# Hybrid decoder layer on one core: how the low pieces of the attention weights are divided between VectorE and GpSimd

## The chip, the cores and the metric

The kernel runs on one core of a Trainium2 chip. The metric is the device time of one execution in microseconds (us), the median of several runs. Engines are TensorE (PE in the profile; PEld are its weight loads), VectorE (DVE), ScalarE (ACT), GpSimd (POOL) and SyncE (SP, which issues most DMAs).

## What is computed

One layer of a decoder over 4096 tokens of width 1024: a normed and modulated input is projected, its columns feed three mixers (forgetting attention with 8 heads of 64, an RWKV-7 recurrence, a pooling), and their gated outputs are projected back. The change lies in the attention alone, whose reference is:

```python
log_f = jax.nn.log_sigmoid((f_logit + f_bias).astype(jnp.float32))
cum = jnp.cumsum(log_f, axis=1).transpose(0, 2, 1)
for i in range(S // Q_BLOCK):                     # 32 blocks of 128 queries
    s = jnp.einsum('bhqd,bhkd->bhqk', qh[:, :, q0:L], kh[:, :, :L])
    s = s + cum[:, :, q0:L, None] - cum[:, :, None, :L]
    p = jax.nn.softmax(jnp.where(causal, s, -jnp.inf), axis=-1)
    outs.append(jnp.einsum('bhqk,bhkd->bhqd', p, vh[:, :, :L]))
```

## The kernel before

The program has five stages, one behind the other: `prepare`, `project`, `recur`, `attend` and `output`. `recur` also does the attention's first row maxima; `attend` lasts from about 1980 to 3147 us of the profiled span.

`attend` is a loop of four turns, each over two heads. A turn has 16 steps, (head u, block b of 512 queries), and step b has 4(b+1) units, one for each block x of 128 keys: 288 units in a turn. In a unit, `p32` holds exp of the scores, 128 keys x `width[k]` queries. The width is 512 but for the last three units of a step, which lie on the diagonal: 384, 256 and 128. Since every step starts at a multiple of four units, unit number modulo 4 says which diagonal width a unit can have: 1 is 384, 2 is 256, 3 is 128.

For precision the weights are multiplied in two pieces. The high piece is the upper half of each float32 of `p32`, read as bfloat16 in place; the low piece `plo` (float16) is `p32` minus the high piece. It is this subtraction that the change divides anew. In the kernel before, unit k's subtraction is done whole by GpSimd (L2711) unless k % 4 is 2, and then whole by VectorE (L2864, in `lower`).

The order of the work is written out by hand, by engine, with semaphores between them:

- TensorE, for unit k: (a mask on the diagonal, L2789), two products into the scores' bank `psc[k % 2]` (L2791, L2793), which wait for exp of unit k - 2; one product for the row maxima of queries 49 units ahead (L1396, four banks `pm`); sometimes a turned row of bounds (L2748); and then `output(k - 5)` (PV_LAG is 5): for each 128 queries one product with the high piece (L2772) and one with the low piece (L2774). `output` waits for the low piece. Right behind a step's start one `output` is skipped and two are done in the next unit.
- ScalarE: exp of each unit (L2732), and at a step's end two evacuations of the sums (L2724). `p32` and `plo` have eight buffers.
- VectorE, for unit k: perhaps the copy of a turned row (L2842), the maximum over the product for row maxima (L2834), `lower(k - 1)`, perhaps the largest of a row (L2847), and five and six units behind a step's start the result (L2870, L2872) and its scaling (L2877). Once a head, `head_vectors` (L1429 to L1433).
- GpSimd, for unit k: perhaps the sums of a row (L1403, which waits for VectorE's maxima of unit k - 1), perhaps a row's seven small pieces (L1412 to L1423, which wait for L2847), and then the low piece.

Of the kernel before, what the change touches and what calls it, by code (L numbers as in the profile page):

```python
# [23 lines left out]
ALU = mybir.AluOpType  # L24
# [4 lines left out]
P = 128  # L29
# [2538 lines left out]
def attend(nc, a, m):  # L2568
# [5 lines left out]
    with ExitStack() as ctx:  # L2574
# [10 lines left out]
        NP, NM = 8, 4  # L2585
        p32 = sb("p32", [P, NP, BT])
        plo = sb("plo", [P, NP, BT], F16)
# [10 lines left out]
        use, row_use, row_there, NPM, pre, EARLY, PV_LAG, ROW_LAG, COPY_LAG = (  # L2598
            p.use, p.row_use, p.row_there, p.NPM, p.pre, p.EARLY, p.PV_LAG, p.ROW_LAG, p.COPY_LAG)

        def by_pool(n):

            return n % 4 != 2

        pool_units = [k for k in range(NQK) if by_pool(k)]
        dve_units = [k for k in range(NQK) if not by_pool(k)]

        k_in = [sem(f"k_in{j}") for j in range(2)]
        q_in = [sem(f"q_in{j}") for j in range(2)]
# [16 lines left out]
        with nc.Block() as block:  # L2626
# [52 lines left out]
            @block.gpsimd  # L2679
            def _(pool):  # L2680
                pool.sem_inc(m_add.sem, EARLY)
                pool.sem_inc(piece.sem, 6 * EARLY)
                pool.sem_inc(row_d.sem, EARLY)
                with pool.Fori(0, TURNS) as i:
                    def sums(kc):

                        pool.wait_ge(pm_d.sem, pm_d.past(i, pre + use[kc] + len(ahead(kc))))
                        row_sum(nc, m, completes(kc)).then_inc(m_add.sem, 1)

                    def pieces(kc):  # L2690

                        nth = rows_before(kc + 1)
                        side, done = (nth - 1) % 2, nth - 1 - EARLY
                        pool.wait_ge(m_max.sem, m_max.past(i, done + 1))
                        for j in range(6):
                            row_piece(nc, m, j, side).then_inc(piece.sem, 1)
                            pool.wait_ge(piece.sem, piece.past(i, done * 6 + j + 1))
                        row_piece(nc, m, 6, side).then_inc(row_d.sem, 1)

                    for k in range(NQK):  # L2700
                        if complete_at(k - 1):
                            sums(k - 1)
                        if complete_at(k - 3):
                            pieces(k - 3)
                        if not by_pool(k):
                            continue
                        pool.wait_ge(exp_d.sem, exp_d.past(i, k + 1))
                        pool.wait_ge(pv_mm.sem, pv_mm.past(i, k + 1 - NP))
                        hi = p32[:, k % NP, :].bitcast(BF16).rearrange("p (t two) -> p t two", two=2)[:, :, 1]
                        w = width[k]  # L2710
                        nc.gpsimd.tensor_tensor(plo[:, k % NP, 0:w], p32[:, k % NP, 0:w], hi[:, 0:w], ALU.subtract)\  # L2711
                            .then_inc(lo_p.sem, 1)

# [24 lines left out]
            @block.tensor  # L2738
            def _(pe):
                pe.sem_inc(pv_mm.sem, pv_mm.credit)  # L2740
                pe.sem_inc(pm_mm.sem, pre)

                def turn_row(g, nth, side):

                    pe.wait_ge(row_d.sem, nth)
                    turned = pm[g][:, 0, :].bitcast(F16)
                    for t in range(CB):
                        ins = nc.tensor.transpose(turned[:, t * P:(t + 1) * P], mw[:, side, t, :], id16[:])  # L2748
                    ins.then_inc(pm_mm.sem, 1)


                with pe.Fori(0, TURNS) as i:
                    def output(k):

                        s, x = units[k]
                        u, b = STEPS[s]
                        if x == 0:
                            pe.wait_ge(o_ev.sem, o_ev.past(i, s))
                            if b == 0:
                                pe.wait_ge(v_in[u], (i + 1) * 16)  # L2760
                        if by_pool(k):
                            pe.wait_ge(lo_p.sem, lo_p.past(i, pool_units.index(k) + 1))
                        else:
                            pe.wait_ge(lo_v.sem, lo_v.past(i, dve_units.index(k) + 1))
                        d = max(0, x - 4 * b)
                        hi = p32[:, k % NP, :].bitcast(BF16).rearrange("p (t two) -> p t two", two=2)[:, :, 1]
                        for t in range(d, CB):
                            c0 = (t - d) * P
                            o = po[t // 2]
                            oc = (t % 2) * VW  # L2770

                            nc.tensor.matmul(o[:, oc:oc + VW], hi[:, c0:c0 + P], v[u][:, x, 0:VW],  # L2772
                                             start=(x == 0 and t % 2 == 0), stop=False, skip_group_check=True)
                            g = nc.tensor.matmul(o[:, oc:oc + 1 + HD], plo[:, k % NP, c0:c0 + P], v[u][:, x, 0:1 + HD],  # L2774
                                                 start=False, stop=(x == 4 * b + t), skip_group_check=True)
                        g.then_inc(pv_mm.sem, 1)

                    for k, (s, x) in enumerate(units):
                        u, b = STEPS[s]
                        if x == 0:  # L2780
                            pe.wait_ge(pm_d.sem, pm_d.past(i, pre + row_there(s) + 1))
                        d = max(0, x - 4 * b)
                        w = width[k]
                        t0 = b * BT + d * P
                        pe.wait_ge(exp_d.sem, exp_d.past(i, k + 1 - 2))
                        ks = slice(x * P, (x + 1) * P)
                        diag = x >= 4 * b
                        if diag:
                            nc.tensor.matmul(psc[k % 2][:, 0:P], idb[:], mk[:], start=True, stop=False,  # L2789
                                             skip_group_check=True)  # L2790
                        nc.tensor.matmul(psc[k % 2][:, 0:w], ka[u][:, ks], qa[u][:, t0:t0 + w], start=not diag,  # L2791
                                         stop=False, skip_group_check=diag)
                        nc.tensor.matmul(psc[k % 2][:, 0:w], kb[u][:, ks], qb[u][:, t0:t0 + w], start=False,  # L2793
                                         stop=True, skip_group_check=diag).then_inc(qk_mm.sem, 1)
                        for j, item in enumerate(ahead(k)):
                            ua, ba = STEPS[item[0]]
                            if ba == 0 and item[1] == 0:

                                nth = i + 1 if ua == 1 else i + 2
                                pe.wait_ge(q_in[ua], nth * 80)  # L2800
                                pe.wait_ge(k_in[ua], nth * 96)
                                pe.wait_ge(fac_in, 32)
                            n = pre + use[k] + j
                            pe.wait_ge(pm_d.sem, pm_d.past(i, n + 1 - NM))
                            query_maximum(nc, m, pm[n % NM][:, 0, :], qa[ua], ka[ua], item).then_inc(pm_mm.sem, 1)
                        if complete_at(k - ROW_LAG):
                            nth = rows_before(k - ROW_LAG + 1)
                            n = pre + use[k] + len(ahead(k))
                            pe.wait_ge(pm_d.sem, pm_d.past(i, n + 1 - NM))
                            turn_row(n % NM, i * NS + nth, (nth - 1) % 2)  # L2810
                        if k - PV_LAG in start[1:NS]:
                            continue
                        if k - (PV_LAG + 1) in start[1:NS]:
                            output(k - (PV_LAG + 1))
                        if k >= PV_LAG:
                            output(k - PV_LAG)
                    for k in range(NQK - PV_LAG, NQK):
                        output(k)

            @block.vector  # L2820
            def _(dve):
# [27 lines left out]
                with dve.Fori(0, TURNS) as i:  # L2849
# [6 lines left out]

                    def lower(k):

                        if not by_pool(k):
                            w = width[k]  # L2860
                            dve.wait_ge(exp_d.sem, exp_d.past(i, k + 1))
                            dve.wait_ge(pv_mm.sem, pv_mm.past(i, k + 1 - NP))
                            hi = p32[:, k % NP, :].bitcast(BF16).rearrange("p (t two) -> p t two", two=2)[:, :, 1]
                            tt(plo[:, k % NP, 0:w], p32[:, k % NP, 0:w], hi[:, 0:w], ALU.subtract).then_inc(lo_v.sem, 1)  # L2864

                    def result(s):

# [17 lines left out]
                    for k, (s, x) in enumerate(units):  # L2885
                        if complete_at(k - COPY_LAG):
                            sr = completes(k - COPY_LAG)
                            n = pre + row_use[sr]
# [311 lines left out]
```

## Time and profile before

| | |
|---|---|
| median of 3 runs | 3571.12 us (3542.68, 3571.12, 3572.24) |
| the profiled execution | 3542.35 us |
| its span, from first to last instruction | 3540.6 us |
| mean granted clock of TensorE | 0.963 of full speed |
| busy: TensorE, VectorE, ScalarE, GpSimd | 3298.0, 2428.2, 1965.7, 1785.6 us |

The busy times are of the whole span. An instruction that is issued and held up by another engine's use of the memory counts as busy. A row of a view names line, engine and operation, the tiles written and read, and their shapes; the bracket or the last column of a row is the idle time of the engine in front of the instruction, and what ended it. Matmuls overlap in the trace: the ends of a matmul are modelled, and the distance between two starts is what one takes.

### The profile page before, as it was taken

The page shows a single profiled execution, that of the slowest core. Times are in us where ns is not written, and L with a number is a line of the kernel's source. Part 1 is how long each engine was busy: PE and PEld are TensorE (multiplying, and loading weights), DVE is VectorE, ACT ScalarE, POOL GpSimd, SP SyncE. Part 2 cuts the span into 40 slices and gives each one's busy share as a digit, 9 for nine tenths or more (in the row PEclk, how much of TensorE's full clock was granted, in tenths as well). Part 3 has the DMA queues.
Part 4 walks back from the last instruction along what each step waited for, and adds up shares of the span by engine and source line. Part 5 has one row for each costly group of instructions (what it writes and reads, how often), then busy time and mean ns, then how long its engine had stood idle before and what let it go on. Part 6 is the DMA issues. An engine that isn't in the chain of part 4 may idle for free. (4 is left out here: it accounts for less than half of the span.)

```text
span 3540.6 us, 90103 instructions
## 1 busy us (share of the span) xinstructions
PE 3298.0 (93%) x31944; PEld 2282.0 (64%) x31944; DVE 2428.2 (69%) x4339; ACT 1965.7 (56%) x3745; POOL 1785.6 (50%) x2083
## 2 busy tenths in 40 slices
PE   6788999999999995999999899999999999979998
PEld 6783489459549742888888466566666666644444
DVE  5797756326533334788775889899899988965454
ACT  2444544325432234577774677677777777753333
POOL 2376400410230043254544798889889889852222
PEclk9898999999999997899998899999999999989999
DMA  7387435344444542232223202022020220215555
GB/s 317 129 303 254 167 128 190 131 149 159 159 143 152 169 155 82 63 86 79 65 53 74 52 16 59 10 56 59 9 58 10 57 58 7 60 70 190 188 185 178
DMA packets 247420, 401.09 MB, mean 113 GB/s; under 512 B 85549, under 2 KB 198916, under 8 KB 231844
## 3 DMA queue, kind: packets, MB, share of 16 engines
q1 hardware_dynamic: 223627, 383.75, 34.0%
q10 hardware_dynamic: 22880, 11.54, 1.3%
q8 instruction: 258, 4.23, 0.5%
q14 instruction: 175, 1.43, 0.1%
q0 software_dynamic: 480, 0.14, 0.1%
HBM read 272.77 MB, written 122.59 MB: 112 GB/s over the span
## 5 line engine op out<-in xcount | busy, mean ns | idle before, releaser
L2732 ACT ACTIVATE p<-psc,seam,sc 128x512 f32<-128x512 f32 (+3 forms) x1152 | 848.6, 743 | 283.1 <-PE psc L2793 270.2
L2711 POOL TENSOR_TENSOR plo<-p 128x512 f16<-128x512 f32 (+2 forms) x864 | 905.5, 1076 | 72.7 <-ACT p L2732 71.5
L2834 DVE TENSOR_REDUCE seam<-pm 128x1 f32<-128x512 f32 (+3 forms) x1152 | 703.5, 637 | 92.4 <-PE pm L1396 80.6
L646 PE MATMUL bank<-h,ring 128*128 128x512 f16 x2688 | 598.4, 381 | 4.5 <-DVE u L990 4.5
L651 PE MATMUL bank<-ring,h 128*128 128x128 f16 x8064 | 468.2, 222 | 25.5 <-ACT c L818 12.3
L646 PEld LDWEIGHTS bank<-h,ring 128*128 128x128 f16 x2688 | 264.1, 98 | 343.1 <-issue 43.0
L651 PEld LDWEIGHTS bank<-ring,h 128*128 128x128 f16 x8064 | 464.7, 99 | 27.0 <-issue 13.0
L1165 POOL CAST stage<-c 128x512 f16<-128x512 f32 x64 | 47.2, 738 | 767.5 <-DVE c L1006 767.5
L3036 PE MATMUL pz<-wo,yh 128*128 128x512 f16 x1024 | 305.6, 380 | 3.1 <-DVE yl L3068 3.1
L2864 DVE TENSOR_TENSOR plo<-p 128x512 f16<-128x512 f32 (+1 forms) x288 | 288.1, 1000 | 0.0
L1000 DVE TENSOR_TENSOR c<-bank,u 128x512 f32<-128x512 f32 x168 | 115.7, 689 | 249.3 <-PE bank L646 171.0
L2772 PE MATMUL po<-v,p 128*128 128x129 f16 x2112 | 255.9, 220 | 11.9 <-POOL plo L2711 10.3
L2772 PE MATMUL po<-seam,p 128*128 128x129 f16 x2112 | 257.5, 220 | 9.6 <-POOL plo L2711 8.0
L2774 PE MATMUL po<-seam,plo 128*128 128x65 f16 x2112 | 242.3, 192 | 0.0
L2774 PE MATMUL po<-v,plo 128*128 128x65 f16 x2112 | 241.0, 192 | 0.0
L2772 PEld LDWEIGHTS po<-v,p 128*128 128x128 bf16 x2112 | 194.2, 97 | 63.0 <-POOL plo L2711 15.9
L2772 PEld LDWEIGHTS po<-seam,p 128*128 128x128 bf16 x2112 | 194.7, 97 | 59.4 <-POOL plo L2711 12.4
L2980 POOL TENSOR_TENSOR o<-o,xr 128x1024 f32<-128x1024 f32 x32 | 75.2, 2352 | 311.9 <-DVE o L3091 311.9
L2774 PEld LDWEIGHTS po<-seam,plo 128*128 128x128 f16 x2112 | 189.6, 98 | 49.5
L2774 PEld LDWEIGHTS po<-v,plo 128*128 128x128 f16 x2112 | 189.6, 98 | 46.8
L2791 PE MATMUL psc<-seam 128*128 128x512 f16 (+1 forms) x576 | 213.0, 370 | 0.1
L1396 PE MATMUL pm<-seam 128*128 128x512 f16 (+3 forms) x576 | 212.7, 369 | 0.0
(430 smaller groups left out, 6837.2 us busy)
## 6 DMA issues: line engine op xcount, KB each, us to landing
ring<-scratch_ws SPq DMA_DIRECT2D x52, 1792.0 KB, 7.9
scratch_z<-stage SPq DMA_DIRECT2D x72, 256.0 KB, 3.1
scratch_ws<-h SPq DMA_DIRECT2D x10, 1792.0 KB, 6.9
y<-scratch_y SPq DMA_DIRECT2D x35, 512.0 KB
g<-scratch_g SPq DMA_DIRECT2D x35, 512.0 KB
xr<-in_x SPq DMA_DIRECT2D x34, 512.0 KB, 6.1
scratch_g<-stage SPq DMA_DIRECT2D x64, 256.0 KB, 6.2
scratch_qk<-stage SPq DMA_DIRECT2D x64, 256.0 KB, 2.6
```

The costliest lines, as they stand in the source:

```text
L646: t = nc.tensor.matmul(bank[b][:], m.ring[:, slot, l, bo, k, :], hh[:, side, r, ao, k, :], start=fresh and first, stop=last, skip_group_ch ...
L651: t = nc.tensor.matmul(bank[b][:, ts], hh[:, side, l, ao, k, ts], m.ring[:, slot, r, bo, k, :], start=fresh and first and tp == 0, stop=la ...
L1000: tt(c[:, t % NC, :], bank[2 if i == 5 else 3][:], (u2 if i == 3 else u1)[:], ALU.add).then_inc(c_dve, 1)
L1396: return nc.tensor.matmul(bank[:, 0:w], qa[:, j * P:(j + 1) * P], ka[:, q * BT:q * BT + w], start=not last, stop=True, skip_group_check=last)
L2711: nc.gpsimd.tensor_tensor(plo[:, k % NP, 0:w], p32[:, k % NP, 0:w], hi[:, 0:w], ALU.subtract)\
L2732: nc.scalar.activation(p32[:, k % NP, 0:w], psc[k % 2][:, 0:w], ACT.Exp, bias=xb[:, u, b, x // 4:x // 4 + 1], scale=m.sc[:, 0:1]).then_inc ...
L2772: nc.tensor.matmul(o[:, oc:oc + VW], hi[:, c0:c0 + P], v[u][:, x, 0:VW], start=(x == 0 and t % 2 == 0), stop=False, skip_group_check=True)
L2774: g = nc.tensor.matmul(o[:, oc:oc + 1 + HD], plo[:, k % NP, c0:c0 + P], v[u][:, x, 0:1 + HD], start=False, stop=(x == 4 * b + t), skip_gro ...
L2791: nc.tensor.matmul(psc[k % 2][:, 0:w], ka[u][:, ks], qa[u][:, t0:t0 + w], start=not diag, stop=False, skip_group_check=diag)
L2834: nc.vector.tensor_reduce(mx[:, s, t, q:q + 1], pm[g][:, 0, 0:w], AX.X, ALU.max).then_inc(pm_d.sem, 1)
L2864: tt(plo[:, k % NP, 0:w], p32[:, k % NP, 0:w], hi[:, 0:w], ALU.subtract).then_inc(lo_v.sem, 1)
L3036: mm = nc.tensor.matmul(pz[u % 2][j][:], l[:, u % 2, k // 4, ks], r[:, k, j * HALF:(j + 1) * HALF], start=(k == 0 and c == 0), stop=(k == ...
```

## The change

GpSimd now works on every unit, on all but the last 128 columns of it (on the 128 where the width is 128); VectorE does the last 128 columns of every unit that is wider than 128. `output` on TensorE waits for both. Buffers, lags and the order of all other work stay as they are.

```diff
-        def by_pool(n):
-            return n % 4 != 2
-        pool_units = [k for k in range(NQK) if by_pool(k)]
-        dve_units = [k for k in range(NQK) if not by_pool(k)]
+        def pool_width(k):
+            return width[k] - P if width[k] > P else P
+        pool_units = list(range(NQK))
+        dve_units = [k for k in range(NQK) if width[k] > P]
...
@@ GpSimd
-                        if not by_pool(k):
-                            continue
                         pool.wait_ge(exp_d.sem, exp_d.past(i, k + 1))
                         pool.wait_ge(pv_mm.sem, pv_mm.past(i, k + 1 - NP))
-                        w = width[k]
+                        w = pool_width(k)
                         nc.gpsimd.tensor_tensor(plo[:, k % NP, 0:w], p32[:, k % NP, 0:w], hi[:, 0:w], ALU.subtract)\
                             .then_inc(lo_p.sem, 1)
...
@@ TensorE, output(k)
-                        if by_pool(k):
-                            pe.wait_ge(lo_p.sem, lo_p.past(i, pool_units.index(k) + 1))
-                        else:
+                        pe.wait_ge(lo_p.sem, lo_p.past(i, k + 1))
+                        if width[k] > P:
                             pe.wait_ge(lo_v.sem, lo_v.past(i, dve_units.index(k) + 1))
...
@@ VectorE, lower(k)
-                        if not by_pool(k):
-                            w = width[k]
+                        if width[k] > P:
+                            ws = slice(width[k] - P, width[k])
-                            tt(plo[:, k % NP, 0:w], p32[:, k % NP, 0:w], hi[:, 0:w], ALU.subtract).then_inc(lo_v.sem, 1)
+                            tt(plo[:, k % NP, ws], p32[:, k % NP, ws], hi[:, ws], ALU.subtract).then_inc(lo_v.sem, 1)
```

## Rows read from the trace of the kernel before

**Rows 1.** The page's first part: busy us, share of the span, instructions.

```profile
PE 3298.0 (93%) x31944; PEld 2282.0 (64%) x31944; DVE 2428.2 (69%) x4339; ACT 1965.7 (56%) x3745; POOL 1785.6 (50%) x2083
```

**Rows 2.** Windows, the second and the last turn: us, busy (count) by engine, clock.

```profile
core 0: us, PE busy (x) PEld busy (x) DVE busy (x) ACT busy (x) POOL busy (x), PEclk, DMA share, GB/s
2273.80:2567.20 293.40, 282.65 (x3170) 183.86 (x3169) 265.73 (x446) 219.31 (x321) 257.96 (x344) 0.99 0.17 39
2860.60:3147.20 286.60, 280.03 (x3140) 182.08 (x3138) 263.23 (x441) 218.59 (x318) 255.99 (x342) 0.99 0.17 39
```

**Rows 3.** Timeline of TensorE, a quiet stretch: start us, us, instruction.

```profile
2505.14 0.38 PE L2791 MATMUL psc<-qa,ka 128*128 128x512 f16 x1
2505.36 0.38 PE L2793 MATMUL psc<-qb,kb 128*128 128x512 f16 x1
2505.57 0.38 PE L1396 MATMUL pm<-ka,qa 128*128 128x512 f16 x1
...
2506.14 0.38 PE L2791 MATMUL psc<-qa,ka 128*128 128x512 f16 x1
```

**Rows 4.** Waits of the attention stage, 1980 to 3150 us: total, times, longest.

```profile
POOL plo L2711 <- ACT p L2732: 71.5, 87, 8.4
PEld po L2772 <- POOL plo L2711: 28.3, 56, 0.8
POOL seam L1403 <- DVE seam L2834: 24.7, 32, 1.0
...
PEld pm L2748 <- POOL seam L1423: 17.4, 24, 1.0
POOL seam L1412 <- DVE seam L2847: 16.8, 16, 1.1
...
PEld po L2772 <- DVE plo L2864: 7.8, 16, 0.8
```

**Rows 5.** Groups by line and shape in the second turn: count, busy, mean ns, idle before.

```profile
L2711 POOL TENSOR_TENSOR plo<-p 128x512 f16<-128x512 f32 x184 | 207.4, 1153 | 17.0 <-ACT p L2732 16.7
L2834 DVE TENSOR_REDUCE seam<-pm 128x1 f32<-128x512 f32 x240 | 158.7, 682 | 17.1 <-PE pm L1396 15.1
L2864 DVE TENSOR_TENSOR plo<-p 128x512 f16<-128x512 f32 x56 | 61.4, 1097 | 0.0
L2711 POOL TENSOR_TENSOR plo<-p 128x384 f16<-128x384 f32 x16 | 13.2, 825 | 0.0
L2864 DVE TENSOR_TENSOR plo<-p 128x256 f16<-128x256 f32 x16 | 10.6, 662 | 0.0
L2834 DVE TENSOR_REDUCE seam<-pm 128x1 f32<-128x128 f32 x16 | 4.5, 278 | 0.5 <-DVE seam L1433 0.5
```

**Rows 6.** The lines of the low pieces, 2000 to 3100 us: duration ns min/median/max.

```profile
L2711 POOL TENSOR_TENSOR plo<-p x817: 394/1038/1561, 1999.4 to 3098.7; 128x512 f16<-128x512 f32 x139, 128x128 f16<-128x128 f32 x13, 128x384 f16<-128x384 f32 x12
L2864 DVE TENSOR_TENSOR plo<-p x272: 408/1009/1597, 2000.8 to 3099.2; 128x512 f16<-128x512 f32 x106, 128x256 f16<-128x256 f32 x30
```

**Rows 7.** Timelines of GpSimd and VectorE where two low pieces meet.

```profile
2652.51 1.04 POOL L2711 TENSOR_TENSOR plo<-p 128x512 f16<-128x512 f32 x1 [0.79 <-ACT p L2732]
2652.59 1.51 DVE L2864 TENSOR_TENSOR plo<-p 128x512 f16<-128x512 f32 x1
2653.51 1.49 POOL L2711 TENSOR_TENSOR plo<-p 128x512 f16<-128x512 f32 x1
```

**Rows 8.** Timeline of VectorE: one lone piece; behind the start of a step.

```profile
2290.17 0.67 DVE L2864 TENSOR_TENSOR plo<-p 128x512 f16<-128x512 f32 x1
...
2359.13 1.51 DVE L2864 TENSOR_TENSOR plo<-p 128x512 f16<-128x512 f32 x1
2360.56 1.27 DVE L2834 TENSOR_REDUCE seam<-pm 128x1 f32<-128x512 f32 x2
2361.76 0.16 DVE L2870 RECIPROCAL rl<-oev 128x4 f32<-128x4 f32 x1
2361.84 0.97 DVE L2872 TENSOR_TENSOR osb<-oev 128x256 f32<-128x256 f32 x1
2362.74 0.68 DVE L2834 TENSOR_REDUCE seam<-pm 128x1 f32<-128x512 f32 x1
2363.34 0.67 DVE L2877 SCALAR_TENSOR_TENSOR osb<-osb,sc,rl 128x256 f32<-128x256 f32 x1
2363.93 0.68 DVE L2834 TENSOR_REDUCE seam<-pm 128x1 f32<-128x512 f32 x1
2364.54 0.92 DVE L2864 TENSOR_TENSOR plo<-p 128x512 f16<-128x512 f32 x1
```

## The prediction

> **What bounds the kernel now.** I read the page's totals first: TensorE is busy for 93% of the span [rows 1]. The change touches only the attention stage, so everything after that is read there: four turns of a loop, two heads and 288 units of work in each. A turn lasts 293.4 us (the last 286.6), with TensorE busy for 282.7, VectorE for 265.7 and GpSimd for 258.0 of it [rows 2]. So three engines are close to full. The timeline of one quiet stretch gives TensorE's own pace: from one unit's first product to the next unit's 1.00 us (2505.14, 2506.14) [rows 3]. That is what it needs, as its matmuls follow each other without a gap. 240 full units at 1.00 and 16 times the three narrow ones of a step (some 2.0 us together by their columns, at 0.21 to 0.22 us for 512 [rows 3]) make 272; 7 of the 293.4 us are the loop's end, which the last turn doesn't have (293.4 - 286.6) [rows 2]. So some 14 us of a turn are left for masks, turned rows and all waits.
>
> The list of waits then says what TensorE waits for in the stage [rows 4]. Its weight loads wait for GpSimd's low piece for 28.3 us (56 times, 0.5 us each), for VectorE's low piece for 7.8 us (16 times) and for the bound row that GpSimd prepares (L1423) for 17.4 us (24 times). That is 53.5 us of 3540.6: all that the change could win directly, 1.5%. In all the other units the low piece has been there for long, since products with it come five units later (PV_LAG). A wait arises only after a pause: GpSimd waits for VectorE before a row (24.7 and 16.8 us) [rows 4], does seven small pieces, and then has a backlog; VectorE has its own after the results of a step [rows 8].
>
> **The change, part by part.** In a turn 216 low pieces of GpSimd (184 of 512 columns, 16 of 384, 16 of 128) become 288 (240 of 384, 16 of 256, 32 of 128), and 72 of VectorE (56 of 512, 16 of 256) become 272 of 128. The number of elements stays the same; GpSimd's share of a full unit becomes even.
>
> What one costs alone: GpSimd 1.04 us at 512 columns, 0.825 at 384, 0.39 at 128 at least [rows 5 to 7]. VectorE 0.67 at 512 columns (2290.17, while GpSimd did only small pieces [rows 8]) and 0.41 at 256, the least of all its low pieces [rows 6]; the reduction of 512 is as long, 0.68 [rows 5]. The reduction of 128 columns takes 0.278 [rows 5], and I take the same for a low piece of 128. In a queue each starts some 0.06 us before the end of the one in front (two reductions in 1.27 and not 1.36 us [rows 8]), so it occupies VectorE for 0.22 us.
>
> What two cost that meet: VectorE's piece that began at 2652.59, just after GpSimd's at 2652.51, ended at 2654.10, 0.55 us after GpSimd's end (2653.55). GpSimd's next, issued at 2653.51, ended at 2655.00, 0.90 us after VectorE's [rows 7]. They ran one after the other, and the later one took nearly its whole length again. So in a queue a 512 piece of VectorE takes 0.55 of the common time and a piece of 128 about 0.15 (0.55 less 384 columns at 1.04 ns, the slope between 0.67 and 0.41). GpSimd's takes 0.90 behind one of VectorE, 1.00 behind its own, and 0.69 at 384 columns (0.90 less the 0.21 between 1.04 and 0.825).
>
> Four full units, both engines in a backlog: before 0.55 + 0.90 + 2 x 1.00 = 3.45 us; after 4 x (0.69 + 0.15) = 3.36. Both are under TensorE's 4.00, and the reduction (0.60) that VectorE does between two pieces fits under GpSimd's 0.69. A backlog thus goes down by 0.16 us a unit in place of 0.14. At TensorE's pace GpSimd is busy 0.8 of each 1.0 us, and VectorE's piece comes into the gap behind it: it waits some 0.25 us for that (1.00 - 0.60 - 0.15), which costs nothing as the cover is TensorE's unit. If VectorE has more than that to do, the cover is gone, and that is the second rival.
>
> The stretch with the tightest wait on VectorE is a step's start. From 2359.13 to 2365.46 it spends 6.33 us there on two low pieces (1.51 and 0.92), four reductions and two result operations [rows 8]. After the change it does five low pieces there of 0.15 to 0.45 us, 0.75 to 2.25 in place of 2.43: earlier by 0.2 to 1.7 us. So VectorE, though it gets 200 more instructions a turn, isn't later at its worst place.
>
> The sum against the profiled execution (3542.35 us, span 3540.6). The last GpSimd piece before each of the 56 waits is 0.21 us shorter: -12 us. A faster way out of the backlog, 0.02 us over some five units, 56 times: -5. The running maximum of a row (L2847) now stands behind one low piece more on VectorE, and GpSimd's row pieces and the row's transposition (24 waits) behind it: 24 x 0.22 = +5 (bounds: 0, and 24 x 0.85 = 20 if each also waits for a whole GpSimd piece). Waits for VectorE's pieces now arise in every unit: between -7.8 (all gone) and +22 (7.8 x 272/72 less 7.8), I take 0, as the two effects above oppose each other. TensorE gets one more wait per unit, 1088 in all; its queue runs ahead under 0.64 us of three long matmuls, in which it issues the present wait for a low piece without a gap [rows 3], so 0 (bounds 0 and 1088 x 0.03 = 33 us). Sum -12 us: 3530 against the profiled 3542.35. The three runs shown lie at 3542.68, 3571.12 and 3572.24, so that execution is one of the lower level; set against the median of 3571.12 the same -12 gives **3559 us**.
>
> **The rivals.** (a) All waits on low pieces vanish, since each unit gets its two pieces at about the same time and neither engine has a 1.5 us instruction left [rows 6]. For it: 1561 and 1597 ns as longest, which can't arise from 0.83 and 0.28. Against: the pauses of GpSimd stay. It gives -28.3 - 7.8 - half of 17.4 = -45 us: 3526, faster by 1.3%.
>
> (b) VectorE becomes the bound. Its 265.7 us hold 61.4 + 10.6 = 72 of low pieces [rows 2, 5], so 193.7 of other work. 272 pieces at 0.22 make 253.5 us, 40 under the turn. But the pieces don't run alone: the 512 form takes 1.097 on average, 0.42 over its own, and the 256 form 0.662, 0.25 over its own [rows 5, 6]. From 0.15 us of true delay per piece on, VectorE exceeds 293.4 ((293.4 - 193.7)/272 = 0.37). At 0.25 it needs 193.7 + 272 x 0.47 = 321.5 us: +28 a turn, +112 in all, 3683, slower by 3.1%. At 0.42 it would be +74 a turn, 3.8 times as many meetings each as dear as today. Against it: what a piece waits is the rest of GpSimd's, which now is shorter and, as worked out above, under 0.1 us in a backlog, and a wait at TensorE's pace is slack that doesn't add up.
>
> The Trainium skill (SBUF — State Buffer, "Who interferes with whom") has a rule for this: a VectorE instruction with two SBUF inputs and a GpSimd instruction that reads SBUF exclude each other for the whole instruction, and whoever comes first blocks the other fully. The trace agrees (0.55 and 0.90 us behind the other's end [rows 7]). The rule speaks against a division by columns, as every unit now has such a meeting and not every fourth; read without the phases it is rival (b), read with them it is my sum.
>
> (c) The change does nothing for the time: the waits come from the pauses alone, and the new split only moves them between the engines. 3571, the same.
>
> **How the numbers follow.** A difference of 1% is about what a measurement of this kernel can tell. My forecast and (c) together 0.57 (0.42 and 0.15), both within 1%, with an own range of 3535 to 3595. (a) 0.18, of which a few land within 1% and are made up for by my forecast's better end: faster 0.2. (b) 0.25, from just over TensorE's pace (+10 a turn, 3611) to 3683; the part under 1% is small: slower 0.23. The range leaves out the far half of (b) and the best of (a): 3515 to 3650.
>
> **What the profile would show.** VectorE's low pieces of 128 at 0.28 to 0.5 us with at most 0.9 as longest, GpSimd's 384 form at 0.83 to 0.98; a four-unit stretch still at 4.0 us on TensorE; 28.3 us of waits for GpSimd's piece down to 10 to 15, those for VectorE's up to some 10. VectorE busy for over 270 us of a turn, since its waits count as busy; that alone is no sign of (b). (b) shows as TensorE waiting for VectorE's pieces in most units and turns of 300 us and more, with GpSimd then idle. The prediction is wrong if a piece of 128 occupies VectorE for over 0.37 us where it has no slack, if GpSimd takes the gap first again and again, or if the extra wait on TensorE opens a gap in front of each unit's products.

## The result, and the profile after

The change made the kernel slower: 3583.86 us in the median of 16 runs against 3557.28 of the kernel before in 16 runs, ratio 1.0084 with a 95% interval of 1.0064 to 1.0105. Forecast were 12 us less. The forecast's 3559 lies within 0.7% of the measured 3583.86 only because it was set on the higher median of three runs; the direction is the wrong one. (The three runs shown ahead had a median of 3571.12; more runs put the kernel before at 3557.28.)

The profiled execution has a span of 3589.8 us, 49.2 more than before's. Not all of it is the change. The windows from the first exp of the attention stage to its last give the stage alone; these rows answer to [rows 2].

Windows of the changed kernel, second and last turn: us, busy (count) by engine, clock.

```profile
core 0: us, PE busy (x) PEld busy (x) DVE busy (x) ACT busy (x) POOL busy (x), PEclk, DMA share, GB/s
2300.10:2601.10 301.00, 286.05 (x3170) 182.43 (x3169) 288.66 (x646) 220.09 (x320) 250.74 (x416) 0.99 0.17 38
2902.20:3195.50 293.30, 282.22 (x3137) 180.29 (x3135) 286.09 (x640) 219.32 (x318) 248.59 (x413) 1.00 0.17 38
```

A turn now takes 301.0 us in place of 293.4, and the last 293.3 in place of 286.6. VectorE is busy for 288.7 us of a turn in place of 265.7; GpSimd for 7 less. The whole stage, from these windows:

```profile
1997.20:3195.50 1198.30, 1139.81 (x12635) 727.68 (x12635) 1152.97 (x2577) 879.41 (x1279) 1000.42 (x1661) 0.99 0.17 38
```

and of the kernel before:

```profile
1980.50:3147.20 1166.70, 1127.00 (x12638) 733.09 (x12639) 1060.04 (x1778) 876.33 (x1278) 1029.87 (x1374) 0.99 0.17 39
```

That is 31.6 us more in the stage, near the 26.6 between the medians. The granted clock is 0.99 in both, so it isn't the clock. Another 16.7 lie ahead of it (1997.2 against 1980.5), in code that is the same; over all profiles of this study that part ends between 1980.5 and 2025.2 us. So below, kernels are compared by the attention stage, from one profile each; its two middle turns agree within 1.1 us in every profile, and the one kernel that was profiled twice gave stages 1.9 us apart (1153.9 and 1155.8). A difference of a few us in the stage is thus no more than a hint. The ratio of times, always against the kernel before, stands beside it where it was taken.

The waits of the changed kernel, 1980 to 3200 us (total, times, longest), answer to [rows 4]. "Issue" is idle time for which the view names nobody.

```profile
POOL plo L2709 <- ACT p L2730: 83.6, 174, 8.4
PEld pm L1396 <- DVE seam L2831: 51.6, 95, 1.4
POOL seam L1403 <- DVE seam L2831: 51.0, 32, 2.4
PEld po L2769 <- issue: 30.4, 89, 1.0
POOL seam L1412 <- DVE seam L2844: 26.7, 40, 1.5
PEld po L2769 <- DVE plo L2861: 24.8, 107, 0.3
...
PE pm L1396 <- DVE seam L2831: 18.4, 38, 0.9
...
PE po L2769 <- POOL plo L2709: 10.6, 28, 0.5
```

Three waits for VectorE have grown: TensorE's for its low piece, 24.8 (7.8 before), TensorE's for its maxima to free a bank, 51.6, and GpSimd's own for VectorE ahead of a row, 51.0 and 26.7 (24.7 and 16.8 before). Before, the bank's wait and the row without a name were small:

```profile
PEld pm L1396 <- DVE seam L2834: 6.3, 20, 0.4
PEld po L2772 <- issue: 12.3, 44, 0.3
PE po L2772 <- POOL plo L2711: 18.3, 48, 0.6
```

TensorE's weight loads waited for GpSimd's low piece for 28.3 us before, and that row is no longer in the list. The wait itself is still there. `output` now waits first for GpSimd's piece and then for VectorE's, and where the first of the two ended the idle time the view has no name for it. This is one of the 89 cases (weight load, GpSimd's piece and VectorE's piece of the same unit):

```profile
2403.96 0.10 PEld L2769 LDWEIGHTS po<-seam,p 128*128 128x128 bf16 x1 [0.58 <-issue]
2402.97 0.88 POOL L2709 TENSOR_TENSOR plo<-p 128x384 f16<-128x384 f32 x1
2402.07 0.28 DVE L2861 TENSOR_TENSOR plo<-p 128x128 f16<-128x128 f32 x1
```

VectorE's piece ended at 2402.35, GpSimd's at 2403.85, and the load began 0.11 us later. Going through all first loads of a unit in this way, 19.8 of the 30.4 us (56 times) end with GpSimd's piece; so TensorE's wait for GpSimd fell from 28.3 to 19.8 us. The matmuls tell the same: 18.3 before, 10.6 after. A weight load's wait passes in part under running matmuls (51.6 us for the banks, of which the matmuls' own row shows 18.4), so these rows don't add up to the loss.

Groups by line and shape, 1980 to 3200 us (busy, mean ns), answer to [rows 5]:

```profile
L2709 POOL TENSOR_TENSOR plo<-p 128x384 f16<-128x384 f32 x960 | 807.0, 864 | 88.0 <-ACT p L2730 79.5 <-PE po L2771 4.7
L2831 DVE TENSOR_REDUCE seam<-pm 128x1 f32<-128x512 f32 x960 | 651.4, 680 | 12.3 <-PE pm L1396 7.8
L2861 DVE TENSOR_TENSOR plo<-p 128x128 f16<-128x128 f32 x1088 | 442.1, 406 | 0.4 <-ACT p L2730 0.4
L2874 DVE SCALAR_TENSOR_TENSOR osb<-osb,sc,rl 128x256 f32<-128x256 f32 x64 | 55.4, 866 | 0.1
```

VectorE's piece takes 406 ns on average; its least and its median, and those of the scaling of a result (answering to [rows 6]) show where the rest comes from:

```profile
L2861 DVE TENSOR_TENSOR plo<-p x1026: 274/310/906, 2020.6 to 3149.3; 128x128 f16<-128x128 f32 x171
L2874 DVE SCALAR_TENSOR_TENSOR osb<-osb,sc,rl x60: 471/1043/1045, 2032.2 to 3142.0; 128x256 f32<-128x256 f32 x60
```

274 ns is the piece alone. 906 is one that waited for a whole piece of GpSimd. Now look at the timelines of the two engines in two stretches. Where GpSimd has a backlog (seven pieces without a gap in 5.87 us):

```profile
2377.62 5.87 POOL L2709 TENSOR_TENSOR plo<-p 128x384 f16<-128x384 f32 x7
```

```profile
2378.33 0.31 DVE L2861 TENSOR_TENSOR plo<-p 128x128 f16<-128x128 f32 x1
2378.56 0.68 DVE L2831 TENSOR_REDUCE seam<-pm 128x1 f32<-128x512 f32 x1
2379.16 0.31 DVE L2861 TENSOR_TENSOR plo<-p 128x128 f16<-128x128 f32 x1
```

VectorE does one unit in 0.83 us. And where GpSimd follows exp at TensorE's pace:

```profile
2355.17 0.83 POOL L2709 TENSOR_TENSOR plo<-p 128x384 f16<-128x384 f32 x1 [0.17 <-ACT p L2730]
2356.17 0.83 POOL L2709 TENSOR_TENSOR plo<-p 128x384 f16<-128x384 f32 x1 [0.17 <-ACT p L2730]
```

```profile
2355.67 0.47 DVE L2861 TENSOR_TENSOR plo<-p 128x128 f16<-128x128 f32 x1
2356.07 0.68 DVE L2831 TENSOR_REDUCE seam<-pm 128x1 f32<-128x512 f32 x1
2356.67 0.47 DVE L2861 TENSOR_TENSOR plo<-p 128x128 f16<-128x128 f32 x1
```

Here the reduction ends while GpSimd's piece of the next unit holds the memory, and VectorE's waits for its end: 2356.00, then 0.14 us of its own. The cycle is 1.00 us. VectorE has no idle time in it, and yet gains nothing on TensorE, though it is late: around this stretch (2345 to 2363 us) TensorE's loads wait five times for VectorE's piece (1.0 us) and twice for a bank (1.0 us).

### The profile page after: what moved, and what is told of

The parts are those of the page before. It is cut to its first block and busy times, and to the rows that moved or that the text cites. A ratio compares the mean times of both kernels' runs of the same rounds, so it can differ in the third digit from the quotient of the medians.

```text
span 3589.8 us, 93363 instructions
## 1 busy us (share of the span) xinstructions
PE 3331.4 (93%) x31944; PEld 2292.7 (64%) x31944; DVE 2519.3 (70%) x5139; ACT 1972.6 (55%) x3745; POOL 1756.0 (49%) x2371
## 5 line engine op out<-in xcount | busy, mean ns | idle before, releaser
L2709 POOL TENSOR_TENSOR plo<-p 128x384 f16<-128x384 f32 (+2 forms) x1152 | 897.1, 803 | 97.0 <-ACT p L2730 83.6
L2831 DVE TENSOR_REDUCE seam<-pm 128x1 f32<-128x512 f32 (+3 forms) x1152 | 729.3, 636 | 30.1 <-PE pm L1396 23.2
L2861 DVE TENSOR_TENSOR plo<-p 128x128 f16<-128x128 f32 x1088 | 442.1, 406 | 0.4 <-ACT p L2730 0.4
L1396 PE MATMUL pm<-ka,qa 128*128 128x512 f16 (+2 forms) x576 | 208.3, 362 | 10.0 <-DVE seam L2831 10.0
```

The costliest lines, as they stand in the source:

```text
L1396: return nc.tensor.matmul(bank[:, 0:w], qa[:, j * P:(j + 1) * P], ka[:, q * BT:q * BT + w], start=not last, stop=True, skip_group_check=last)
L2831: nc.vector.tensor_reduce(mx[:, s, t, q:q + 1], pm[g][:, 0, 0:w], AX.X, ALU.max).then_inc(pm_d.sem, 1)
L2861: tt(plo[:, k % NP, ws], p32[:, k % NP, ws], hi[:, ws], ALU.subtract).then_inc(lo_v.sem, 1)
```

## Experiments

Theory 1 is that VectorE falls behind, by its meetings with GpSimd (1a) or by the fixed cost of 200 more instructions a turn (1b), and TensorE waits for it. Theory 2 is that the extra wait on TensorE opens a gap in each unit. Each edit is to `attend`. The kernels with 64, 192 and no columns on VectorE and with remainders 3 and 0 were run once, with the profile; the others were timed as well.

**A second wait, in the kernel before.**

```diff
+                        if k % 4 != 2 and k >= 4:
+                            pe.wait_ge(lo_v.sem, lo_v.past(i, dve_units.index(k - k % 4 + 2 - 4) + 1))
+                        elif k >= 4:
+                            pe.wait_ge(lo_p.sem, lo_p.past(i, pool_units.index(k - 3) + 1))
```

> The kernel before, with nothing changed but a second, always long met wait on TensorE in front of each unit's products (on the other engine's latest low piece of an earlier unit). Theory 1 (VectorE falls behind, and TensorE waits for it): the attention stage stays at 1166.7 us and the time at before's, ratio 1.000. Theory 2 (the extra wait opens a gap on TensorE in each unit): up to 1136 x 0.03 us = 34 us more, ratio near 1.008, all of what the change cost.

Measured: ratio 1.0018 (0.9983 to 1.0052), stage 1172.6 us, 5.9 more than before. The turns took 297.0, 294.6, 295.3 and 285.7, so this is uneven and may be smaller. By the stage, theory 2 explains a fifth of the 31.6 us; the ratio's interval alone would allow some 18 us (0.0052 of 3557). The two runs with a one-input instruction below bound it better.

**A one-input instruction in place of VectorE's piece, in the changed kernel.** `plo` is cleared once ahead of the loop.

```diff
-                            tt(plo[:, k % NP, ws], p32[:, k % NP, ws], hi[:, ws], ALU.subtract).then_inc(lo_v.sem, 1)
+                            nc.vector.tensor_reduce(junk[:, k % NP:k % NP + 1], p32[:, k % NP, ws], AX.X, ALU.max).then_inc(lo_v.sem, 1)
...
```

> The changed kernel, with VectorE's subtraction in each unit replaced by a maximum over the same 128 columns into a scratch column: as long (0.28 us alone) but with one input in SBUF. It leaves out the low pieces of the last 128 columns (they are zero). Theory 1a (VectorE is late since each piece waits for the rest of GpSimd's, 406 ns on average against 276 alone): the instruction falls to 0.28 us, VectorE gets 272 x 0.13 = 35 us of a turn back, the waits for the row maxima's banks (51.6 us) nearly vanish, and the stage goes from 1198 to 1165 or less. Theory 1b (200 more instructions a turn, each with its fixed cost, are what fills VectorE): the stage stays over 1185. Theory 2 (TensorE's extra wait): stays at 1198.

Measured: ratio 0.9861 (0.9804 to 0.9917), stage 1125.4 us, 72.9 less than the changed kernel. The instruction took its own length each time, and the waits for VectorE's maxima nearly went, as rows of this run show:

```profile
L2866 DVE TENSOR_REDUCE junk<-p 128x1 f32<-128x128 f32 x1088 | 297.8, 274 | 0.0
PEld pm L1396 <- DVE seam L2836: 0.8, 3, 0.3
POOL seam L1403 <- DVE seam L2836: 5.8, 8, 1.0
```

As many instructions, of the same length, on the same engine, and the loss is gone twice over. That is 1a, and it speaks against 1b. The edit takes away one of two inputs and also the write of 128 columns (it writes one); which of the two makes the meeting is not told apart here.

**The same in the kernel before**, over the whole width of every fourth unit.

> The kernel before, with VectorE's subtraction (every fourth unit whole) replaced by a maximum over the same columns, one input in SBUF. It leaves out the low pieces of those units (they are zero). It shows what the meetings of the two engines cost before the change. If each of the change's meetings is dear since there are four times as many, the stage falls here by much less than the 73 us that the same edit gave in the changed kernel: by 15 to 35 us, to about 1140. If the price goes by columns and not by meetings, it falls by as much as there. The difference to the 1125 us of the changed kernel without meetings is then what the even division is worth by itself.

Measured: ratio 0.9892 (0.9832 to 0.9953), stage 1121.0 us, 45.7 less than before.

```profile
L2869 DVE TENSOR_REDUCE junk<-p 128x1 f32<-128x512 f32 x224 | 151.1, 675 | 0.0
L2714 POOL TENSOR_TENSOR plo<-p 128x512 f16<-128x512 f32 x736 | 759.6, 1051 | 148.3 <-ACT p L2735 142.5
```

VectorE's took 675 ns in place of 1097, GpSimd's 1051 in place of 1153. So the meetings cost 45.7 us before and 72.9 after; my range of 15 to 35 for before was too low. Without them the two divisions differ by 4.4 us (1125.4 against 1121.0). The 31.6 us of the change are thus 27.2 of meetings and 4.4 of all else, TensorE's second wait among it, as the first of these two kernels has it and the second has not. A piece of VectorE was issued while one of GpSimd's ran 224 times in 288 before and 816 times in 1088 after: a meeting cost the stage some 0.20 us before and 0.09 after (45.7/224 and 72.9/816).

**No low piece on VectorE at all**, GpSimd as after the change: the condition of `lower` is false and TensorE's wait for it is left out.

> The changed kernel without any low piece on VectorE, GpSimd as after the change. It leaves out the low pieces of the last 128 columns. It shows what VectorE's pieces cost altogether, waits and instructions. With the one-input instruction in place the stage was 1125 us; if the number of instructions costs little once nothing meets, it is 1110 to 1125 here, if it costs much, under 1100. TensorE's own need, 272 to 275 us a turn with the loop's end, is the floor.

Measured: stage 1118.4 us. 272 instructions fewer on VectorE a turn give only 7.0 us against the run with the one-input instruction. 1118 to 1121 is what the rest of the stage needs, VectorE's results still meeting GpSimd.

**Every second unit, 256 columns.** VectorE's width is now a function of its own, and `pool_width` is the unit's width less this one:

```diff
+            return min(2 * P, width[k] - P) if k % 2 == 0 else 0
```

> The same share of columns divided otherwise: VectorE takes 256 columns of every second unit (k even), GpSimd the rest, so VectorE has about half as many low pieces as after the change (0.41 us alone in place of twice 0.28) and half as many meetings with GpSimd. Theory 1 (VectorE's occupation): it wins back 136 x (2 x 0.22 - 0.35) = 12 us of VectorE a turn and about half of the lock waits, so the stage should lie between the two kernels, 1170 to 1188. Theory 2: half of the extra waits remain, 1182.

Measured: ratio 1.0035 (0.9997 to 1.0072), stage 1180.4 us, between the two kernels, which both theories allow: by itself it tells nothing apart.

**64 and 192 columns on VectorE in each unit**, by the same function.

```diff
+            return 64 if width[k] > P else 0
```

```diff
+            return min(192, width[k] - P) if width[k] > P else 0
```

> The changed kernel with 64 columns on VectorE in place of 128 in each unit, and 448 on GpSimd: as many low pieces on VectorE, half the elements. If VectorE's part in a meeting is the wait for GpSimd's rest (now 0.93 us long in place of 0.83), its piece gets no shorter than 0.35 us on average and the stage stays within 1185 to 1215. If VectorE's own columns count, it gains 272 x 0.07 = 18 us a turn on VectorE and the stage falls under 1180.

> The changed kernel with 192 columns on VectorE and 320 on GpSimd in each unit: the counterpart of the run with 64 (stage 1219.0; 1198.3 with 128). Theory 1 (VectorE, once late, gets one piece in per GpSimd piece and stays late): GpSimd's piece is 0.11 us shorter, VectorE's own 0.07 us longer; in a GpSimd backlog the cycle stays at 0.83 us or just over, and at TensorE's pace VectorE's piece lies in a wider gap. With the trend from 64 to 128 the stage would go on down, to 1180 to 1195. If what counts is VectorE's sum (272 x 0.07 = 18 us a turn more on an engine busy for 288.7 of 301), it goes up, to 1215 or more.

Measured: stages of 1219.0 and 1192.1 us, with 1198.3 at 128. The groups of these two runs:

```profile
L2715 POOL TENSOR_TENSOR plo<-p 128x448 f16<-128x448 f32 x960 | 881.2, 948 | 42.3 <-ACT p L2736 39.1
L2868 DVE TENSOR_TENSOR plo<-p 128x64 f16<-128x64 f32 x1088 | 448.8, 413 | 0.4 <-ACT p L2736 0.4
```

```profile
L2715 POOL TENSOR_TENSOR plo<-p 128x320 f16<-128x320 f32 x960 | 752.3, 806 | 111.8 <-ACT p L2736 101.9 <-PE po L2778 6.6
L2868 DVE TENSOR_TENSOR plo<-p 128x192 f16<-128x192 f32 x1024 | 428.7, 419 | 0.4 <-ACT p L2736 0.4
```

VectorE's piece takes 413, 406 and 419 ns on average at 64, 128 and 192 columns. Its own columns don't show in this average: it takes what GpSimd's rest leaves. Taking half of VectorE's work away made the stage 20.7 us longer, as GpSimd's piece got longer. That acts in two ways which this run doesn't separate: VectorE waits longer in each meeting, and GpSimd itself is late. Its low piece was the later of the two in some 49 us of TensorE's waits here, against 19.8 at 128 columns, though the list puts most of that down to VectorE:

```profile
PEld po L2776 <- DVE plo L2868: 79.3, 265, 0.7
```

For 64 columns the first expectation was the nearer, but 1219.0 is 4 us over its end; that for 192 held.

**The largest of a row first.**

```diff
+                        if complete_at(k - 2):
+                            largest(k - 2)
                         if k:
                             lower(k - 1)
-                        if complete_at(k - 2):
-                            largest(k - 2)
```

> The changed kernel with the largest of a row (L2844) ahead of the low piece in VectorE's order, 64 times in all. If the late rows (GpSimd waits 26.7 us for L2844 and then has a backlog) carry a good part of the loss, the stage falls by 5 to 15 us. If the banks of the row maxima and VectorE's lag as such carry it, it falls by 0 to 3, as VectorE's sum stays. Theory 2: unchanged at 1198.

Measured: ratio 1.0077 (1.0039 to 1.0115), stage 1194.8 us, 3.5 less than the changed kernel. GpSimd's wait for L2844 fell from 26.7 to 17.6 us, but its wait for the maxima stayed at 51.0. The late largest carries at most a small part of the loss: the expectation for that case was 0 to 3 us, and 3.5 is less than twice what two profiles of one kernel differed by (1.9).

**Another phase, in the kernel before.** Whole units by turns as before, but VectorE on other ones: `n % 4 != 1`, then 3 and 0, and 1 once more.

> The kernel before with one number changed: VectorE takes the units with k % 4 = 1 whole, not those with 2. GpSimd does the small pieces of a row in front of a unit with k % 4 = 1, and it is this unit's low piece for which TensorE waits in the kernel before. With VectorE on it, GpSimd has one unit more of time behind each row. Expected: waits for GpSimd's piece from 28.3 to 10 to 18 us, the stage from 1166.7 to 1150 to 1160, ratio 0.995 to 0.998. If VectorE is late there in its place, no gain.

> The kernel before, VectorE taking the units with k % 4 = 3 whole. Those units come two behind the one in front of which GpSimd does a row's small pieces, so GpSimd gets less help where it is late; the diagonal unit it gives up is the one of 128 columns, so it has 16 x 128 columns a turn more. Expected: stage 1165 to 1180, no gain, if the gain of the units with remainder 1 (1153.9) comes from the place behind the row and not from any move.

> The kernel before, VectorE taking the units with k % 4 = 0 whole, right ahead of the unit with the row's small pieces. GpSimd is free for a unit before its pause. VectorE gets all of its 72 units full (512 columns). Expected: stage 1150 to 1170: the gain of remainder 1 in part, less 16 x 256 columns a turn more on VectorE.

> The kernel with VectorE on the units with k % 4 = 1 once more, for its interval: the first time the ratio was 0.9969 with an interval over 1, the stage 1153.9 us, 12.8 less than before. Expected: the stage within 1 us of 1153.9, ratio 0.995 to 0.998.

Measured: with remainder 1 a stage of 1153.9 and 1155.8 us in its two runs, ratio 0.9969 (0.9929 to 1.0009) and 0.9961 (0.9930 to 0.9992); with remainder 3 1168.4, with 0 1160.8; with 2, the kernel before, 1166.7. The waits with remainder 1:

```profile
PEld pm L2748 <- POOL seam L1423: 17.4, 16, 1.2
PEld po L2772 <- POOL plo L2711: 16.0, 36, 0.9
```

28.3 us became 16.0. All of these expectations held but that of the repeat, whose stage missed its 1 us by 0.9. Remainder 1 is faster than both kernels, by about 12 us in the stage and some 0.3 to 0.4% of the whole, at the edge of what the runs tell.

## Why the prediction was wrong

**What held.** VectorE's piece costs what was worked out: 0.274 us alone against 0.278; 0.83 us a unit in a backlog against 0.84; at TensorE's pace a wait that fills the cycle to 1.00 us, which I had as 0.25 and which is some 0.2 (0.47 against 0.27). The extra wait on TensorE was taken as 0 with 33 us as bound; no row shows the 0.03 us apiece behind that bound. Measured were 5.9 us for 1136 waits, and no more than 4.4 net, with all else, between the two kernels without meetings.

**The step that failed** is that VectorE's piece "waits some 0.25 us for that (1.00 - 0.60 - 0.15), which costs nothing as the cover is TensorE's unit". The sentence behind it, that the cover is gone if VectorE has more to do, named the case, and I put it aside as a rival. It is what happened. After each step VectorE has a result to compute and to scale, and once a head its vectors; it is then late and must gain on TensorE. Followed unit by unit through the trace, its piece ends 3 to 5 us behind exp through most of the steps of 12, 16 and 20 units; in a step of 20, 4.9 us behind in its seventh unit, it is still 4.1 behind in its nineteenth, where before it came down from 3.3 to 1.5, and with the one-input instruction from 3.1 to 1.4. Where GpSimd follows exp at TensorE's pace, each piece of a late VectorE meets one of GpSimd's, and it gets exactly one in per piece of GpSimd (the timeline at 2355.67 and 2356.67), so it stays late until GpSimd has a backlog itself. Before, three reductions in four had no meeting behind them, and four units cost VectorE some 3.5 us (four times 0.60 and one piece of 1.10) to TensorE's 4.0. The one-input runs show the size: 72.9 us of stage go with the meetings alone, 27.2 more than before.

**The terms of the sum.** Waits for VectorE's pieces, taken as 0 between -7.8 and +22, were +17.0 (24.8 less 7.8). The banks of the row maxima stood in no term, though VectorE frees them and the wait was there with 6.3 us; it grew by 45. GpSimd's waits ahead of a row, taken as +5, grew by 36 us (51.0 and 26.7 for 24.7 and 16.8), though not all of it reaches TensorE. For GpSimd's piece I had -12 and -5, and the wait fell by 8.5 (28.3 to 19.8), half of that, while GpSimd's own waits for VectorE grew.

**The start of a step.** I had VectorE 0.2 to 1.7 us earlier there. From the start of the piece of the third unit to the end of that of the seventh it was 6.33 us [rows 8] and is 6.03 (2389.12 to 2395.15). So this stretch came out at the near end of what I had. The five short pieces did save time, but the scaling of the result, now right behind a low piece, finds GpSimd's next one holding the memory: 1.04 us in place of 0.67. And it was not the worst place. In the step of 12 units the same stretch went from 5.63 us (from 2290.17) to 6.83 (2316.19 to 2323.02), and TensorE then waited for VectorE's piece:

```profile
2393.04 0.31 DVE L2861 TENSOR_TENSOR plo<-p 128x128 f16<-128x128 f32 x1
2393.27 1.04 DVE L2874 SCALAR_TENSOR_TENSOR osb<-osb,sc,rl 128x256 f32<-128x256 f32 x1
2394.24 0.68 DVE L2831 TENSOR_REDUCE seam<-pm 128x1 f32<-128x512 f32 x1
2394.84 0.31 DVE L2861 TENSOR_TENSOR plo<-p 128x128 f16<-128x128 f32 x1
...
2322.50 0.52 DVE L2861 TENSOR_TENSOR plo<-p 128x128 f16<-128x128 f32 x1
2323.07 0.10 PEld L2769 LDWEIGHTS po<-seam,p 128*128 128x128 bf16 x1 [0.34 <-DVE plo L2861]
```

**The rivals.** (a) was wrong: both waits for low pieces are still there, 19.8 and 24.8 us. (b) had the right mechanism at under a third of its price (31.6 us of 112): the pieces took 0.13 us over their own, not 0.25, and the point from which VectorE fills a whole turn (0.15) was not reached. The kernel got slower all the same, since VectorE need not be full on average: it is enough that it can't catch up between two steps. The rule of the Trainium skill (SBUF — State Buffer, "Who interferes with whom"), read without phases, pointed the right way, and my reading with phases the wrong way. The same section says that a VectorE instruction with at most one SBUF input, outside the two-port modes, doesn't contend with GpSimd. The run with one SBUF input agrees: 274 ns on average over 1088 instructions, the length alone.

How the loss of 27.2 us divides between VectorE's delay and GpSimd's (whose 384 form took 864 ns on average, 842 with the one-input instruction) was not measured apart, nor how much of VectorE's delay reaches TensorE by way of a late GpSimd, nor what of the other 4.4 is TensorE's wait.

## What to carry to other kernels

Where two engines exclude each other for the length of an instruction, count the meetings, not the elements: one long piece in four units left VectorE three units to catch up in, four short ones left it none at TensorE's pace. A meeting has no fixed price, though: here it was half as dear when there were 3.6 times as many. A wait is slack only for an engine that is on time; ask how it gets back once it is late, and price every resource that it frees, not only the one that the change edits. Where a consumer waits for two producers, a row of waits that disappears may only have lost its name; look at which producer ended last. Where the work is divided by turns, try whose turn it is first: moving it by one unit gained some 0.3 to 0.4% here, at the edge of what the runs tell, and dividing it anew lost 0.8%.

## What the hardware showed

VectorE's piece took 406 to 419 ns on average at 64, 128 and 192 columns, beside GpSimd pieces of 448, 384 and 320: with a piece of both in each unit, the length of the shorter instruction hardly showed. The meetings of the kernel before, which looked like a normal 1097 ns of an instruction, cost 45.7 us of its stage, more than all waits for low pieces in its list together (28.3 and 7.8).
